# Six row dots moved from the end of the upward phase into the first six items of the downward phase

## The chip, the core and the metric

The kernel runs on one core of a Trainium2 chip. The metric is the time of one execution on the device, in microseconds (us). The engines named below are PE (TensorE: matrix products), DVE (VectorE) and ACT (ScalarE) for elementwise work, POOL (GpSimd), which here issues gathers and stores, and SP (SyncE), which issues the other transfers. Each engine runs its own list of instructions in order; semaphores order work between them. Sixteen DMA engines serve all transfers.

## What is computed

The reference is one step of a decoder layer for 520 tokens (512 of a prompt, 8 samples) of width 1024: modulated norm, a recurrent block and sparse attention, an output projection, then a feed-forward with 16384 experts and a last norm. The change touches the feed-forward alone:

```
s = jnp.einsum('nhpd,hpkd->nhpk', q, subkeys)        # two top-16 lists per head, 8 heads
e = ...                                              # 128 chosen experts for each token
g = jax.nn.softmax(best, axis=-1)
z = jnp.einsum('nd,nhkd->nhk', xc, u_tab[e])         # token times chosen rows of u
act = (jax.nn.gelu(z.astype(jnp.float32)) * g).astype(xc.dtype)
return jnp.einsum('nhk,nhkd->nd', act, v_tab[e])     # weighted sum of chosen rows of v
```

## The kernel before

The feed-forward is done in two ways at once.

**Dense part, 392 tokens.** For all 16384 experts, in 128 blocks of 128, PE computes u times the hidden state (upward phase, `up(b)`, b = 0 to 127), ACT applies GeLU, and the results go to memory. Then, in the downward phase, they are read back, multiplied by a gate that is zero where a token did not choose an expert, and multiplied by v (`down(k)`, k = 0 to 127, accumulated over all k in the eight banks of PE's accumulator memory). One block is called an item. Each 32-bit product is made of three passes of reduced width: high times high, high times low, low times high. So every item needs a high and a low part of its weights, 128x1024 (`raw` -> `uh` by ACT in `high(i)`, then `ul = raw - uh` by DVE in `low(i)`; i = 0 to 127 are blocks of u, 128 to 255 blocks of v) and, downward, of the gated activations (`zin` times the gate `gr` in `gate_item`, `ah` by ACT in `high_a`, `al` by DVE in `low_item`). Rings of four buffers hold `raw`, `uh`/`ul`, `zbuf`, `zin`, `ah`/`al`.

**Sparse part, the other 128 tokens.** One token stands in each partition. For each of its 128 choices, POOL gathers the token's row of u (128 rows of 1024, 512 KB per gather) and DVE multiplies and sums it with the token's hidden state: `dot_rows(n)`, the row dot, which fills column n of `zg`. When all 128 columns are there, ACT applies GeLU (`ag`), DVE multiplies by the softmax weight (`gwt`), POOL gathers rows of v, and DVE adds them up, `add_rows(n)`: vacc += row * ag[n]. The gathers share one ring of four buffers (`xT` in the profile): the gather of u row n waits for dot n-4, the gather of v row n for dot 124+n (n < 4) or for sum n-4.

**What sets the order around the change.** In the last part of the upward phase PE alternates `up` with `quad` products that build the gate; ACT moves them to `stage`, and POOL stores them to `gw` in seven chunks. The last chunk's four stores (3.5 MB) stand in POOL's list behind the gather of u row 121 and ahead of that of row 122. After the last quad PE runs only `up(122)` to `up(127)`, then `down(0)` on. `up(b)` waits for `low(b)`; ACT, after it has taken `up(b)` out, does `high(b + 4)`. DVE's list there is `low(i)` for i = 123 to 127, with two dots (122, 123; 124, 125; 126, 127) behind each of the first three. On SP, the load of raw block i waits for `low(i - 4)`; behind the load of raw block 130 come the wait for all stores of `gw`, the loads of `gr` for items 0 to 3 and of `zin` for item 0, and later those of the next items. At item 8 the saved residual (2 MB, `xspill`) is read in the same list.

Of the kernel before, what the change touches and what calls it, by code (L numbers as in the profile page):

```python
# [16 lines left out]
ACT = mybir.ActivationFunctionType  # L17
AX = mybir.AxisListType
ADD, MUL, SUB, MAX, MIN, EQ = ALU.add, ALU.mult, ALU.subtract, ALU.max, ALU.min, ALU.is_equal

P = 128
# [26 lines left out]
NCH = DN // TC  # L48
# [6 lines left out]
TILE_G = (0, 6, 6, 6, 2)  # L55
PLACED = 8
FIRST_L = (0, 1, 2, 3, PLACED, 4, 5, 6)
CH_U, CH_G = 9, 14
LAST_G = sum(TILE_G) + NCH * CH_G + 4
TAIL_U = 6  # L60
HOT_U = Q_U + sum(TILE_U)
JB = 4
# [29 lines left out]
def build(nc, io):  # L92
    ctx = ExitStack()
    with ctx:
        def sem(name):
            return ctx.enter_context(nc.semaphore(name))

        def sb(name, shape, dt=F32):
            return ctx.enter_context(nc.sbuf_tensor(name, shape, dt))
# [24 lines left out]
        gwt, zg, ag = sb("gwt", [P, P]), sb("zg", [P, P]), sb("ag", [P, P])  # L124
# [141 lines left out]
        S = {n: sem(n) for n in names}  # L266
# [199 lines left out]
        def _(pool):  # L466
# [55 lines left out]
            def gather(n, table, s):  # L522
                pool.indirect_dma_start(  # L523
                    out=gb[:, s, :], out_offset=None, in_=table,
                    in_offset=bass.IndirectOffsetOnAxis(ap=gidx[:, n:n + 1], axis=0)).then_inc(gb_l[s], 16)

            def store_stage(ch, q):

                pool.wait_ge(S["g_moved"], QPC * (ch + 1))
                cols = slice(q * P * TC // PIECES, (q + 1) * P * TC // PIECES)  # L530
                pool.dma_start(io["gw"][ch, :, cols], stage[:, ch % 2, cols]).then_inc(st_l[ch % 2], 16)
# [5 lines left out]
            for n in range(P):  # L537
                if n >= 4:
                    pool.wait_ge(S["ttr_done"], n - 3)
                gather(n, io["u"], n % 4)  # L540
                if n in after_gather:
                    store_stage(*after_gather[n])
                if n == LAST_G - 1:
                    for q in range(PIECES):
                        store_stage(NCH - 1, q)
            v = io["v"].rearrange("a b d -> (a b) d")
# [575 lines left out]
        def _(act):  # L1122
# [8 lines left out]
            def fn(out, in_, f, **kw):  # L1131
                return act.activation(out, in_, f, **kw)  # L1132
# [48 lines left out]
            for n in range(1, ZC):  # L1181
# [12 lines left out]
                b = 2 * (n % 2)  # L1194
# [76 lines left out]
            def high(i):  # L1271

                act.wait_ge(raw_l[i % 4], 16 * (i // 4 + 1))
                if i >= 4:
                    act.wait_ge(S["pe_item"], i - 3)
                fn(uh[:, i % 4, :], raw[:, i % 4, :], ACT.Copy).then_inc(S["hi_done"], 1)

            def gelu(b, bank):
                act.wait_ge(S["pe_item"], b + 1)
                if b >= 4:  # L1280
                    act.wait_ge(zst[b % 4], 16 * (b // 4))
                fn(zbuf[:, b % 4, :], ps[:, bank, 0:DN], ACT.Gelu_apprx_tanh).then_inc(S["gelu_done"], 1)
                high(b + 4)
# [54 lines left out]
            for n in range(QUADS):  # L1338
                move_quad(n)
                for q in after_quad(n % QPC, CH_U):  # L1340
                    b = HOT_U + (n // QPC) * CH_U + q
                    gelu(b, b % 4)
            def high_a(k):
                act.wait_ge(S["mul_done"], k + 1)
                fn(ah[:, k % 4, :], zin[:, k % 4, :], ACT.Copy).then_inc(S["ah_done"], 1)
            for b in range(P - TAIL_U, P):
                if b == P - 1:
                    high_a(0)
                gelu(b, b % 4)
                if b == P - 3:  # L1350
                    act.wait_ge(S["ttr_done"], P)
                    fn(ag[:, :], zg[:, :], ACT.Gelu_apprx_tanh).then_inc(S["zg_gelu"], 1)

            for k in range(P):
                if k >= 4:
                    act.wait_ge(S["pe_item"], P + k - 3)
                if k >= 1:
                    high_a(k)
                if 4 <= k + 1 < P:
                    high(P + k + 1)  # L1360
# [7 lines left out]
        def _(dve):  # L1368
            steps = [0]

            def link(*group):

                for ins in group:
                    steps[0] += 1
                    ins.then_inc(S["dve_step"], 1)
                dve.wait_ge(S["dve_step"], steps[0])

            tt, ts, cp = dve.tensor_tensor, dve.tensor_scalar, dve.tensor_copy
# [138 lines left out]
            for n in range(0, ZC, 2):  # L1517
# [3 lines left out]
                b = 2 * (n % 2)  # L1521
# [201 lines left out]
            for c in range(KD):  # L1723
                dve.wait_ge(S["pe_step"], c + 1)
                b = 2 + 2 * (c % 3)
# [35 lines left out]
            def low(i):  # L1761

                dve.wait_ge(S["hi_done"], i + 1)
                tt(ul[:, i % 4, :], raw[:, i % 4, :], uh[:, i % 4, :].bitcast(F32), SUB).then_inc(S["lo_done"], 1)  # L1764
# [44 lines left out]
            def dot_rows(n):  # L1809

                dve.wait_ge(gb_l[n % 4], 16 * (n // 4 + 1))
                dve.tensor_tensor_reduce(gb[:, n % 4, :], gb[:, n % 4, :], hg[:, :], 1.0, 0.0, MUL, ADD,  # L1812
                                         zg[:, n:n + 1]).then_inc(S["ttr_done"], 1)
# [27 lines left out]
            r, m = slice(0, P), P  # L1841
# [104 lines left out]
            for n in range(QUADS):  # L1946
                ch, i = n // QPC, n % QPC
# [3 lines left out]
                    low(HOT_U + 1 + ch * CH_U + q)  # L1951
                for q in after_quad(i, CH_G):
                    dot_rows(sum(TILE_G) + ch * CH_G + q)
            for n in range(LAST_G - 4, LAST_G):
                dot_rows(n)
            def gate_item(k):
                s, jj = k // JB, k % JB
                if jj == 0:
                    dve.wait_ge(g_l[s % 4], 16 * (s // 4 + 1))
                dve.wait_ge(zl[k % 4], 16 * (k // 4 + 1))  # L1960
                z = zin[:, k % 4, :].rearrange("p (c t) -> p c t", t=TC)
                tt(z, z, gr[:, s % 4, :].rearrange("p (c j t) -> p c j t", j=JB, t=TC)[:, :, jj, :], MUL).then_inc(S["mul_done"], 1)  # L1962

            def low_item(k):
                dve.wait_ge(S["ah_done"], k + 1)
                tt(al[:, k % 4, :], zin[:, k % 4, :], ah[:, k % 4, :].bitcast(F32), SUB).then_inc(S["a_ready"], 1)  # L1966
            for i in range(P - TAIL_U + 1, P):
                low(i)
                for n in range(LAST_G, P)[2 * (i - P + TAIL_U - 1):2 * (i - P + TAIL_U)]:
                    dot_rows(n)  # L1970
            gate_item(0)
            low(P)
            low_item(0)
            dve.wait_ge(S["zg_gelu"], 1)
            link(tt(ag[:, :], ag[:, :], gwt[:, :], MUL))


            def add_rows(n):

                dve.wait_ge(gb_l[n % 4], 16 * (P // 4 + n // 4 + 1))  # L1980
                if n == 0:
                    ts(vacc[:, :], gb[:, 0, :], ag[:, 0:1], None, MUL).then_inc(S["acc_step"], 1)
                else:
                    dve.wait_ge(S["acc_step"], n)
                    stt(vacc[:, :], gb[:, n % 4, :], ag[:, n:n + 1], vacc[:, :], MUL, ADD).then_inc(S["acc_step"], 1)  # L1985
            for k in range(P):
                if k:
                    gate_item(k)
                add_rows(k)
                if k:  # L1990
                    low_item(k)
                if P + k + 1 < 2 * P:
                    low(P + k + 1)
# [137 lines left out]
```

## Time and profile before

| | |
|---|---|
| median of 3 runs | 1822.7 us (1821.66 to 1826.14) |
| profiled execution | 1822.52 us, of which the span of the trace is 1820.0 us |
| PE busy | 1746.2 us, 96% of the span |
| DVE, ACT, POOL busy | 72%, 36%, 19% |
| mean granted clock of PE | 0.974 of full speed |
| DMA | 467.85 MB moved, mean 257 GB/s |

Times in the trace count from the start of the span. The upward phase ends at about 1253 us and the downward phase runs from there to about 1792 us. The chain of work that ended last puts 28% of the span on the downward products (line 1089) and 25% on the upward ones (line 979). Matmul rows overlap in the trace, so what one item costs on PE is read from the distance between the ends of items.

### The profile page before, as it was taken

How to read it: one execution, taken by the hardware profiler on the slowest of the kernel's cores; microseconds unless marked ns; L12 is line 12 of the kernel's file. 1: busy time of each engine (PE TensorE's matmuls, PEld its weight loads, DVE VectorE, ACT ScalarE, POOL GpSimd, SP SyncE). 2: the span in 40 equal slices, each digit the busy share in tenths (PEclk: the TensorE clock that was granted, in tenths of full speed). 3: DMA queues.
4: the chain of work that ended last, by engine and by line, in shares of the span. 5: the costliest groups of instructions: out<-in, count | busy, mean ns of one | idle time of the engine just before them, and what ended most of it. 6: DMA issues, size and time to landing. Idle time of an engine off the chain costs nothing.

```text
span 1820.0 us, 30382 instructions
## 1 busy us (share of the span) xinstructions
PE 1746.2 (96%) x11385; PEld 1626.7 (89%) x11385; DVE 1314.0 (72%) x2978; ACT 647.6 (36%) x1023; POOL 341.5 (19%) x372
## 2 busy tenths in 40 slices
PE   7999998779899999999999999998999999999997
PEld 5688876448799999999999999998999999999997
DVE  0224336662676799998999999956787777777776
ACT  1114422661332234343333333332343333333332
POOL 3101000000000002111333333333222222222220
PEclk9999986899899999999999999998999999999999
DMA  9767654300532147776899999989999999999992
GB/s 345 245 220 278 223 162 161 119 1 1 185 126 85 70 129 270 246 234 205 288 364 365 365 348 339 336 314 371 403 395 330 340 342 335 340 339 330 345 309 78
DMA packets 178952, 467.85 MB, mean 257 GB/s; under 512 B 20515, under 2 KB 92707, under 8 KB 177294
## 3 DMA queue, kind: packets, MB, share of 16 engines
q1 hardware_dynamic: 130974, 290.20, 45.9%
q0 software_dynamic: 45120, 173.61, 26.4%
q10 hardware_dynamic: 2736, 2.49, 0.4%
q8 instruction: 68, 1.11, 0.2%
q14 instruction: 54, 0.44, 0.1%
HBM read 408.86 MB, written 64.17 MB: 260 GB/s over the span
## 4 chain that ended last, share of the span: by engine, by line
PE 85%; DVE 6%; DMA 4%; ACT 2%; issue 1%; ACTq 1%; SPq 0%; POOL 0%; DVEq 0%
PE ps L1089 28%; PE ps L979 25%; PE ps L716 6%; PE ps L966 5%; PE ps L1068 5%; PE ps L919 3%; PE ps L618 2%; ACT arena L1132 1%; PE ps L591 1%; DMA xT<-in_u,gidx 1%; DMA arena<-in_w_in 1%; PE ps L895 1%; PE ps L887 1%; DMA raw<-in_v 1%; DVE arena L1630 1%
## 5 line engine op out<-in xcount | busy, mean ns | idle before, releaser
L1764 DVE TENSOR_TENSOR ul<-raw,uh 128x1024 fp32r<-128x1024 f32 x256 | 311.5, 1222 | 117.8 <-ACT uh L1132 116.3
L979 PE MATMUL ps<-hh,uh 128*128 128x392 f32 x1024 | 358.2, 350 | 8.7 <-DVE ul L1764 8.7
L979 PE MATMUL ps<-hl,uh 128*128 128x392 f32 x1024 | 349.8, 342 | 0.0
L979 PE MATMUL ps<-hh,ul 128*128 128x392 f32 x1024 | 349.0, 341 | 0.0
L1089 PE MATMUL ps<-ah,uh 128*128 128x392 f32 x1000 | 339.6, 340 | 2.5 <-DVE al L1966 2.5
L1089 PE MATMUL ps<-ah,ul 128*128 128x392 f32 x1000 | 341.7, 342 | 0.0
L1089 PE MATMUL ps<-al,uh 128*128 128x392 f32 x1000 | 340.9, 341 | 0.0
L1132 ACT ACTIVATE uh<-raw 128x1024 fp32r<-128x1024 f32 x256 | 269.8, 1055 | 105.6 <-PE ps L1089 91.2
L523 POOL DMA_INDIRECT xT<-in_u,gidx x128 | 148.8, 1163 | 585.6 <-DVE zg L1812 370.1
L523 POOL DMA_INDIRECT xT<-in_v,gidx x128 | 132.4, 1034 | 408.7 <-DVE vacc L1985 388.4
L1132 ACT ACTIVATE zbuf<-ps 128x392 f32<-128x392 f32 x128 | 63.7, 498 | 407.0 <-PE ps L979 407.0
L979 PEld LDWEIGHTS ps<-hh,uh 128*128 128x128 f32 x1024 | 193.3, 189 | 10.9 <-DVE ul L1764 9.3
L979 PEld LDWEIGHTS ps<-hl,uh 128*128 128x128 f32 x1024 | 193.3, 189 | 0.0
L979 PEld LDWEIGHTS ps<-hh,ul 128*128 128x128 f32 x1024 | 193.2, 189 | 0.0
L1089 PEld LDWEIGHTS ps<-ah,uh 128*128 128x128 f32 x1000 | 187.9, 188 | 3.2 <-issue 1.9
L1089 PEld LDWEIGHTS ps<-al,uh 128*128 128x128 f32 x1000 | 187.8, 188 | 0.0
L1089 PEld LDWEIGHTS ps<-ah,ul 128*128 128x128 f32 x1000 | 187.7, 188 | 0.0
L1812 DVE CUSTOM_DVE_ANT_0 xT<-xT,hg 128x1024 f32<-128x1024 f32 x128 | 155.2, 1215 | 22.7 <-DMA xT<-in_u,gidx 22.5
L1985 DVE SCALAR_TENSOR_TENSOR vacc<-xT,ag,vacc 128x1024 f32<-128x1024 f32 x127 | 162.3, 1278 | 0.0
L1132 ACT ACTIVATE ah<-zin 128x392 fp32r<-128x392 f32 x128 | 68.2, 532 | 236.9 <-DVE zin L1962 236.9
L716 PE MATMUL ps<-arena 128*128 128x260 f32 x576 | 132.5, 389 | 2.9 <-DVE arena L1418 2.0
L716 PEld LDWEIGHTS ps<-arena 128*128 128x128 f32 x576 | 109.2, 192 | 20.1 <-DMA arena<-in_w_in 3.1
(355 smaller groups left out, 2221.1 us busy)
## 6 DMA issues: line engine op xcount, KB each, us to landing
raw<-in_uT SPq DMA_DIRECT2D x128, 512.0 KB, 5.1
raw<-in_v SPq DMA_DIRECT2D x128, 512.0 KB, 6.3
zs<-zbuf SPq DMA_DIRECT2D x128, 196.0 KB, 5.3
gw<-stage POOLq DMA_DIRECT2D x28, 896.0 KB, 8.9
gr<-gw SPq DMA_DIRECT2D x32, 784.0 KB, 8.3
zin<-zs SPq DMA_DIRECT2D x128, 196.0 KB, 5.8
arena<-in_ada_w SPq DMA_DIRECT2D x32, 512.0 KB, 4.4
arena<-in_w_in SPq DMA_DIRECT2D x18, 512.0 KB, 6.8
```

The costliest lines, as they stand in the source:

```text
L523: pool.indirect_dma_start(out=gb[:, s, :], out_offset=None, in_=table, in_offset=bass.IndirectOffsetOnAxis(ap=gidx[:, n:n + 1], axis=0)).t ...
L618: last = mm(ps[g * HD:(g + 1) * HD, 2 + 2 * c + h, 1 - m:257 - m], w1p[:, c * 16 + m * 8 + j, :], xv[:, h, :, c, g, j, :], start=(m == 0 a ...
L716: last = mm(ps[:, 2 * (n % 2) + h, 0:HALF], win_w[:, (n % 2) * KD + k, :], hT[:, k, h * HALF:(h + 1) * HALF], start=(k == 0), stop=(k == K ...
L919: last = mm(ps[:, 2 + 2 * (c % 3) + h, 0:HALF], wout[:, k, c * P:(c + 1) * P], zT[:, k, h * HALF:(h + 1) * HALF], start=(k == 0), stop=(k ...
L966: last = mm(ps[:, b + h, 0:HALF], weights[w](k), moving[m](k)[:, h * HALF:(h + 1) * HALF], start=(first and n == 0 and w == 0 and m == 0), ...
L979: last = mm(ps[:, bank, 0:DN], w[x][:, k * P:(k + 1) * P], m[:, k, G0:TOK], start=(k == 0 and x == 0 and m is hh), stop=(k == KD - 1 and x ...
L1068: last = mm(ps[:, 4 + n % 4, t * P:(t + 1) * P], oh[:, n % 6, t * P:(t + 1) * P], oh[:, n % 6, (4 + t) * P:(5 + t) * P], start=True, stop= ...
L1089: last = mm(ps[:, dc, 0:DN], w[:, q, cols], m[:, q, :], start=(first and w is uh and m is ah), stop=False)
L1132: return act.activation(out, in_, f, **kw)
L1764: tt(ul[:, i % 4, :], raw[:, i % 4, :], uh[:, i % 4, :].bitcast(F32), SUB).then_inc(S["lo_done"], 1)
L1812: dve.tensor_tensor_reduce(gb[:, n % 4, :], gb[:, n % 4, :], hg[:, :], 1.0, 0.0, MUL, ADD, zg[:, n:n + 1]).then_inc(S["ttr_done"], 1)
L1985: stt(vacc[:, :], gb[:, n % 4, :], ag[:, n:n + 1], vacc[:, :], MUL, ADD).then_inc(S["acc_step"], 1)
```

## The change

`LATE_G` is 6. The last six dots, 122 to 127, leave the upward phase; one stands in each of the items 0 to 5 of the downward phase, in the place where a row sum stood. ACT's GeLU over `zg` moves from behind `up(125)` to item 6. The row sums begin at item 6; from there each item adds one row, and items 19, 39, 59, 79, 99 and 119 add two, so that 128 are added in all. The code of PE, POOL and SP issues the same instructions in the same order.

```
-LAST_G = sum(TILE_G) + NCH * CH_G + 4
+LATE_G = P - sum(TILE_G) - NCH * CH_G - 4
...
@@ ACT @@
-                if b == P - 3:
-                    act.wait_ge(S["ttr_done"], P)
-                    fn(ag[:, :], zg[:, :], ACT.Gelu_apprx_tanh).then_inc(S["zg_gelu"], 1)
             for k in range(P):
                 if k >= 4:
                     act.wait_ge(S["pe_item"], P + k - 3)
+                if k == LATE_G:
+                    act.wait_ge(S["ttr_done"], P)
+                    fn(ag[:, :], zg[:, :], ACT.Gelu_apprx_tanh).then_inc(S["zg_gelu"], 1)
                 if k >= 1:
                     high_a(k)
...
@@ DVE @@
             for i in range(P - TAIL_U + 1, P):
                 low(i)
-                for n in range(LAST_G, P)[2 * (i - P + TAIL_U - 1):2 * (i - P + TAIL_U)]:
-                    dot_rows(n)
             gate_item(0)
             low(P)
             low_item(0)
-            dve.wait_ge(S["zg_gelu"], 1)
-            link(tt(ag[:, :], ag[:, :], gwt[:, :], MUL))
...
+            def added(k):
+                def rows_until(m):
+                    return max(m - LATE_G, 0) + min(m // 20, LATE_G)
+                return range(rows_until(k), rows_until(k + 1)) if k >= LATE_G else ()
             for k in range(P):
                 if k:
                     gate_item(k)
-                add_rows(k)
+                if k < LATE_G:
+                    dot_rows(P - LATE_G + k)
+                if k == LATE_G:
+                    dve.wait_ge(S["zg_gelu"], 1)
+                    link(tt(ag[:, :], ag[:, :], gwt[:, :], MUL))
+                for n in added(k):
+                    add_rows(n)
                 if k:
                     low_item(k)
                 if P + k + 1 < 2 * P:
                     low(P + k + 1)
```

DVE's list at the end of the upward phase, before, from dot 121 on. L1812 is a dot (the second row reads its sum out), L1764 is `low`:

```order
L1812 ISA xT,zg<-xT,hg 128x1024
L1812 ISA zg 128x1
L1764 TENSOR_TENSOR ul<-raw,uh 128x1024
L1812 ISA xT,zg<-xT,hg 128x1024
L1812 ISA zg 128x1
L1812 ISA xT,zg<-xT,hg 128x1024
L1812 ISA zg 128x1
L1764 TENSOR_TENSOR ul<-raw,uh 128x1024
```

The same place after, up to dot 123. L1962 is `gate_item`, L1966 `low_item`:

```order
L1812 ISA xT,zg<-xT,hg 128x1024
L1812 ISA zg 128x1
L1764 TENSOR_TENSOR ul<-raw,uh 128x1024 x5
L1962 TENSOR_TENSOR zin<-zin,gr 128x392
L1764 TENSOR_TENSOR ul<-raw,uh 128x1024
L1966 TENSOR_TENSOR al<-zin,ah 128x392
L1812 ISA xT,zg<-xT,hg 128x1024
L1812 ISA zg 128x1
L1764 TENSOR_TENSOR ul<-raw,uh 128x1024
L1962 TENSOR_TENSOR zin<-zin,gr 128x392
L1812 ISA xT,zg<-xT,hg 128x1024
L1812 ISA zg 128x1
```

Between dot 121 and the first gated item five `low` now stand with nothing between them, and dot 122 stands behind `low_item(0)`.

DVE's list after at items 18 and 19, where the first doubled sum stands (L1980 is the row sum; before, one stood in each item):

```order
L1980 SCALAR_TENSOR_TENSOR vacc<-xT,ag,vacc 128x1024
L1966 TENSOR_TENSOR al<-zin,ah 128x392
L1764 TENSOR_TENSOR ul<-raw,uh 128x1024
L1962 TENSOR_TENSOR zin<-zin,gr 128x392
L1980 SCALAR_TENSOR_TENSOR vacc<-xT,ag,vacc 128x1024 x2
L1966 TENSOR_TENSOR al<-zin,ah 128x392
```

Of the two sums of item 19 the second stands ahead of that item's `low_item`.

## Rows read from the trace of the kernel before

**Rows 1.** The page's first part: busy time, share and instructions by engine.

```profile
PE 1746.2 (96%) x11385; PEld 1626.7 (89%) x11385; DVE 1314.0 (72%) x2978; ACT 647.6 (36%) x1023; POOL 341.5 (19%) x372
```

**Rows 2.** Stages: length, busy time by engine, granted clock, DMA share, GB/s.

```profile
1216.00:1228.00 12.00, 9.52 (x54) 9.19 (x52) 0.00 (x0) 4.33 (x6) 4.02 (x5) 1.00 0.99 403
1228.00:1240.00 12.00, 7.11 (x25) 7.11 (x26) 8.71 (x13) 0.00 (x0) 7.63 (x5) 0.57 0.85 308
1240.00:1254.00 14.00, 13.02 (x73) 12.69 (x71) 4.65 (x7) 5.54 (x9) 1.68 (x1) 1.00 1.02 387
1254.00:1308.00 54.00, 53.36 (x299) 53.35 (x300) 41.31 (x52) 17.41 (x23) 13.85 (x13) 1.00 1.04 403
1308.00:1312.00 4.00, 3.09 (x18) 2.76 (x17) 3.92 (x5) 1.52 (x3) 0.75 (x1) 1.00 1.04 392
...
1400.00:1700.00 300.00, 300.00 (x1682) 300.00 (x1681) 236.05 (x281) 111.50 (x140) 71.42 (x70) 1.00 0.96 338
```

**Rows 3.** Waits from 1210 to 1260 us: total, times, longest, in us.

```profile
DVE xT L1812 <- DMA xT<-in_u,gidx: 21.1, 3, 15.5
...
PE ps L979 <- DVE ul L1764: 7.4, 1, 7.4
...
PE ps L1089 <- DVE al L1966: 1.6, 1, 1.6
```

**Rows 4.** Timeline of DVE, 1200 to 1320 us: start, length, instruction, [idle before].

```profile
1211.30 1.23 DVE L1812 CUSTOM_DVE_ANT_0 xT<-xT,hg 128x1024 f32<-128x1024 f32 x1 [3.49 <-DMA xT<-in_u,gidx]
...
1212.45 1.22 DVE L1764 TENSOR_TENSOR ul<-raw,uh 128x1024 fp32r<-128x1024 f32 x1
1229.20 1.22 DVE L1812 CUSTOM_DVE_ANT_0 xT<-xT,hg 128x1024 f32<-128x1024 f32 x1 [15.54 <-DMA xT<-in_u,gidx]
...
1231.62 1.22 DVE L1764 TENSOR_TENSOR ul<-raw,uh 128x1024 fp32r<-128x1024 f32 x1
...
1252.31 0.57 DVE L1962 TENSOR_TENSOR zin<-zin,gr 128x392 f32<-128x392 f32 x1 [9.35 <-DMA zin<-zs]
...
1254.41 0.28 DVE L1975 TENSOR_TENSOR ag<-ag,gwt 128x128 f32<-128x128 f32 x1
```

**Rows 5.** Timeline of ACT, the same stretch.

```profile
1212.18 1.05 ACT L1132 ACTIVATE uh<-raw 128x1024 fp32r<-128x1024 f32 x1
...
1225.55 0.50 ACT L1132 ACTIVATE zbuf<-ps 128x392 f32<-128x392 f32 x1 [2.85 <-PE ps L979]
...
1240.18 0.50 ACT L1132 ACTIVATE zbuf<-ps 128x392 f32<-128x392 f32 x1 [13.19 <-PE ps L979]
...
1244.47 0.50 ACT L1132 ACTIVATE zbuf<-ps 128x392 f32<-128x392 f32 x1 [2.84 <-PE ps L979]
...
1245.81 0.30 ACT L1132 ACTIVATE ag<-zg 128x128 f32<-128x128 f32 x1
```

**Rows 6.** The chain that ended last, 1200 to 1320 us: start, length, what.

```profile
1214.01 2.18 POOL gw L531 x4
...
1216.49 12.69 DMA xT<-in_u,gidx
...
1242.28 0.38 SPq L424
...
1242.71 9.50 DMA zin<-zs
...
1254.64 34.56 PE ps L1089 x192
```

**Rows 7.** Issue to landing: the last four stores of gw; then three loads of gr.

```profile
DMA to landing us min/median/max: 7.4/9.9/12.2
...
DMA to landing us min/median/max: 9.0/10.7/13.5
```

**Rows 8.** Timeline of DVE in the settled downward phase.

```profile
1604.46 1.23 DVE L1764 TENSOR_TENSOR ul<-raw,uh 128x1024 fp32r<-128x1024 f32 x1 [0.89 <-ACT uh L1132]
...
1606.08 1.28 DVE L1985 SCALAR_TENSOR_TENSOR vacc<-xT,ag,vacc 128x1024 f32<-128x1024 f32 x1
```

More of the change, by code:

```diff
@@ L542, in _ @@
                     store_stage(*after_gather[n])
-                if n == LAST_G - 1:
+                if n == P - LATE_G - 1:
                     for q in range(PIECES):
@@ L1953, in _ @@
                     dot_rows(sum(TILE_G) + ch * CH_G + q)
-            for n in range(LAST_G - 4, LAST_G):
+            for n in range(P - LATE_G - 4, P - LATE_G):
                 dot_rows(n)
```

## The prediction

> **What bounds the kernel now.** I read the page first, then the table of stages, then the waits, timelines and chain around the border of the two phases. PE is busy for 96% of the span [rows 1], so time can only be won where PE is idle or runs at less than full clock. The stages show where that is. From 1400 to 1700 us PE is never idle at full clock: 1682 products in 300 us are 70.1 items of 24, 4.28 us each [rows 2]. In that stage DMA moves 338 GB/s, and since it reaches 403 from 1254 to 1308 us [rows 2], PE is the bound and the transfers have some 16% to spare. Between 1216 and 1254 us it is otherwise: PE lacks 2.5, 4.9 and 1.0 us in three stages, and the granted clock of the middle one is 0.57 [rows 2].
>
> The waits name the cause: PE waited once, 7.4 us, for `low` of DVE, and once, 1.6 us, for `al`; DVE waited 21.1 us in three pieces for gathered rows of u [rows 3]. In DVE's timeline `low(123)` runs at 1212.45, then dot 122 is idle for 15.54 us and starts at 1229.20, and `low(124)` starts at 1231.62 only [rows 4]. Its input was ready long before: ACT wrote `uh` of block 124 from 1212.18 to 1213.23 [rows 5]. PE had ended `up(123)` at 1225.55, when ACT could take it out [rows 5], and needed `low(124)` from then. So the wait of dot 122 is what PE waits for. The chain says why the row was late: four stores to `gw` at 1214.01 come ahead of the gather of row 122, which is issued at 1216.49 and takes 12.69 us [rows 6].
>
> Two prices follow. The stall itself is 7.4 us. After it the clock is at half (1.2 of 2.4 GHz): `up(124)` runs from about 1232.9 (1225.55 plus 7.4) to 1240.18, 7.3 us, while `up(125)` takes 1244.47 - 1240.18 = 4.29 us [rows 5]. The low clock costs 3.0 us.
>
> At the border the chain has the loads of `gr` and `zin` for item 0, issued at 1242.28 and 1242.71, the second landing 9.50 us later; DVE starts on it at 1252.31 [rows 4, 6], and `down(0)` at 1254.64 [rows 6]: 2.43 us from landed data to PE (from 1252.21). Those loads stood in SP's list behind raw block 130, which waits for `low(126)`, itself delayed by the dots.
>
> **The change part by part.**
>
> *Six dots leave the tail.* DVE then goes from `low(123)` straight to `low(124)`, ready about 1214.9 (1212.45 plus two times 1.22). `low(125)`, `low(126)` and `low(127)` follow ACT's `high`, which follow the ends of PE's items, so each is ready at least one item (4.29 us) ahead of PE. PE does not wait: `up(124)` to `up(127)` run from 1225.5 to 1225.5 + 4 x 4.29 = 1242.7. Before, they ended at 1254.64 - 1.6 = 1253.0. Gain up to here 7.4 + 3.0 = 10.4 us. What hid the dots' own 1.22 us before is no matter; they were no price, their waiting was.
>
> *SP's list moves up.* Raw blocks 128, 129 and 130 are no longer held by late `low`s: they are issued at about 1215, 1220 and 1224; before, the first of them had to wait for `low(124)`, over at 1232.8 [rows 4], and the last stood just ahead of 1242.28 [rows 6]. The next wait in that list, which was over long before, is now the one that ends last: the stores of `gw` must have landed. The row I don't have is how long these stores take with the raw loads beside them. Bounds: alone, the last of four was issued at about 1215.7 (1216.19 less a quarter of 2.18) and took at most 12.2 us, so 1227.9 [rows 6, 7]; at worst every byte of the three raw loads and of two stores of z (2.0 MB, in 4.9 us at 403 GB/s) goes first: 1232.8. I take 1232, close to the late bound, since DMA was full from 1216 to 1228 already (share 0.99) [rows 2] and the raw loads need their 1.6 MB somewhere. The loads of `gr` and `zin` for item 0 then land about 9.9 us after issue, as they did under a full DMA [rows 6]: 1241.9, and `down(0)` could start at 1244.3 by the same 2.43 us. PE is ready at 1242.7. It waits some 1.3 to 1.6 us, as before: the wait keeps its length and moves 10 to 11 us forward. Gain from this term 0.3 us. The early bound (1227.9 and 9.0 us) has no wait at all: gain 1.6. The late bound (1232.8, and 13.5 us, the slowest load of `gr` [rows 7]) gives 1246.3 + 2.4 = 1248.7, a wait of 6.0 us, a loss of 4.4 against the old 1.6, and possibly the low clock again, 3.0 more.
>
> *Dots in items 0 to 5.* A dot of 1.22 us stands where a sum of 1.28 (0.75 in item 0, and 0.28 for `ag` times `gwt`) stood [rows 4, 8]. DVE's item gets no longer. The data: rows 122 to 125 were gathered before item 0; 126 and 127 are gathered after dots 122 and 123, four items ahead of their use, as every v row was. Cost nothing; the cover is the ring of four items, 17 us against a landing of 12.69 at the worst seen [rows 6]. POOL issues two gathers of u and four of v later than before: 3.1 MB leave the crowded stretch before `down(0)`.
>
> *GeLU over zg at item 6.* ACT does it (0.30 us [rows 5]) behind the end of `down(2)`, for which it waits anyway, and DVE's 0.28 follows; PE needs item 6 three items later, 12.8 us. Nothing.
>
> *Six doubled items.* One more sum of 1.28 us in each. In the settled phase DVE is idle 0.89 us per item, waiting for ACT, which waits for `down(k-3)` [rows 8]. So DVE has `al` of item k when PE begins `down(k-2)`, two items or 8.5 us ahead, and the 1.28 us are a delay of 0.4 in the next `low`. The second row was gathered with the ring's usual three to four items of lead. Price 0; if that lead were gone, 1.28 - 0.89 = 0.4 us each, 2.3 in all.
>
> *DMA behind the border.* A gain at the border is only kept if transfers keep up. Before, they were full from 1254 to 1312 us at least, and PE lacked 0.9 us at 1308 to 1312 [rows 2]: the 2 MB residual was ahead of a raw block. Check by bytes: the same work up to `down(0)` without 3.1 MB is 7.9 us less at 390 to 403 GB/s, and the DMA time lost while SP and POOL were held (308 instead of 403 GB/s for 12 us, 387 for 14) is 3.4 us more: 11.3 us. So DMA can be 11.3 us earlier at the border and behind it, against PE's 10.7. They agree to within the guess about the stores; the small stall at item 13 stays as it is.
>
> Here a page of the Trainium skill speaks against the change. "SBUF — State Buffer", in the section on a bandwidth-pool intuition, puts memory to one core at some 358 GB/s and calls it the usual end-to-end bottleneck. Rows of this kernel have 403 over 54 us [rows 2], so the measurement decides here and the sum goes by it. By the page's figure the 55 us from `down(0)` to item 13 would carry 2.5 MB less, an estimate of 6 us of stalls and of 1818 for the time, which would fall into rival D below.
>
> **Sum.** 7.4 (stall) + 3.0 (clock) + 0.3 (border) = 10.7 us. Against the profiled execution, 1822.5 - 10.7 = 1811.8 us; that execution lies 0.2 us under the median of the runs, so the median of the changed kernel is forecast at 1811.9, 0.6% less.
>
> **Rivals.**
>
> *A, the forecast*, border wait between 0.5 and 3 us: 1810.5 to 1813.3. Chance 0.55.
>
> *B, all hidden.* Stores land early, no border wait, and the stall at item 13 goes as well: 1822.7 - 7.4 - 3.0 - 1.6 - 0.9 = 1809.8. For it: 3.1 MB fewer in the queues. Against it: the raw loads beside the stores. 0.18.
>
> *C, the wait moves to the border.* The stores and `gr` come by the late bound: gain 10.4 - 4.4 = 6.0, or 3.0 if the clock falls again: 1816.7 to 1819.7. For it: the three loads of `gr` behind the border took 9.0 us or more each [rows 7]. 0.13.
>
> *D, transfers can't feed the earlier start.* PE begins at 1244, and the raw blocks of items 4 to 14 come late. If no more flowed there than the 338 GB/s of the settled stage, the 55 us up to item 13 would carry 3.6 MB less, 9 us: 1820.8; halfway to 403, 4.5 us: 1816.4. For it: DMA is full in the whole stretch behind the border. Against it: it is full because it runs ahead; need is 338, and 403 flow [rows 2]. 0.07.
>
> *E, slower.* The six doubled items: the second sum waits for its gather, `low_item` stands behind it, and DVE's lead of 8.5 us is spent. It ends on the other side of the old time when each costs PE over 10.7 / 6 = 1.8 us; at 4 us each it would be 24 less 10.7: 1835. Against it: gathers are issued three to four items (12.8 us and more) ahead. 0.04.
>
> *F, the change doesn't do what it says.* PE's wait at 1225 is held by something other than the dots, and is still there: 1822. Against it: `uh` of block 124 was ready 12 us earlier [rows 5]. 0.03.
>
> **How the numbers follow.** Within 0.3% (5.5 us, about what a measurement of this kernel can tell from no change) of 1822.7 means 1817.2 to 1828.2. Below it lie A, B, 0.10 of C and 0.03 of D: faster 0.86. The rest of C (with the low clock) and of D, and F, are the same: 0.10. E is slower: 0.04. The range of 8 in 10 takes in A and B and the first values of C and D: 1808.5 to 1817.5, with 1.3 us under B for its own spread; 0.14 is left above it. The likeliest case's own range is 1810.5 to 1813.3.
>
> **What would show it.** In the changed profile: no wait of DVE for a gather between 1213 and 1243; no wait of PE for `low`; granted clock 1.00 from 1216 to 1244; ends of `up(124)` to `up(127)` 4.29 us apart; `down(0)` at 1244 (1242.7 if B, 1248 if C), held by `al`, behind `zin` of item 0, behind the stores; the raw loads of v from 1215 on; dots of 1.22 us in items 0 to 5 without idle time before them; 4.28 us per item at items 19 to 119. A longer border wait, DVE waiting for `uh` behind raw loads in items 4 to 14, or PE idle at item 19 or 39 would prove me wrong.

## The result and the profile after

The changed kernel takes 1808.59 us (median of 5 runs, 1804.13 to 1810.51), the kernel before 1821.66 us (5 runs, 1814.34 to 1826.14). The difference is 13.1 us; the ratio is 0.9927, 95% interval 0.9904 to 0.9950. Run again on another chip the ratio was 0.9938 (0.9920 to 0.9956), which is 11.3 us less. It is faster.

The stages after, with the columns of [rows 2]:

```profile
1216.00:1228.00 12.00, 12.00 (x69) 12.00 (x68) 3.68 (x3) 4.34 (x6) 4.24 (x4) 1.00 1.03 407
1228.00:1240.00 12.00, 12.00 (x69) 12.00 (x69) 0.00 (x0) 4.34 (x6) 0.00 (x0) 1.00 1.03 403
1240.00:1254.00 14.00, 13.72 (x76) 13.24 (x75) 13.93 (x21) 4.53 (x7) 4.75 (x4) 1.00 1.06 393
1254.00:1308.00 54.00, 54.00 (x302) 53.67 (x302) 41.81 (x55) 19.70 (x27) 12.26 (x12) 1.00 1.04 403
1308.00:1312.00 4.00, 4.00 (x25) 4.00 (x24) 4.00 (x6) 1.69 (x3) 1.60 (x2) 1.00 1.04 406
...
1400.00:1700.00 300.00, 300.00 (x1681) 300.00 (x1681) 241.01 (x285) 111.52 (x140) 80.80 (x74) 1.00 0.96 346
```

The three holes of PE in [rows 2] (2.5, 4.9, 1.0 us) have shrunk to one of 0.3 us, the granted clock is 1.00 throughout, and PE is whole at 1308 us too. The last stage carries one doubled item's gather more per 20 items, 346 GB/s, with PE never idle.

The waits after, 1210 to 1260 us, against [rows 3]: the 15 us wait of a dot and PE's wait for `low` are gone. DVE waits for `zin` of item 0 instead, 12.4 us, and PE for `al` 0.3 us:

```profile
DVE zin L1962 <- DMA zin<-zs: 12.4, 1, 12.4
...
DVE xT L1812 <- DMA xT<-in_u,gidx: 3.4, 1, 3.4
...
PE ps L1089 <- DVE al L1966: 0.3, 1, 0.3
```

DVE's timeline after, against [rows 4]: the `low` of blocks 123 and 124 run one behind the other, those of 125, 126 and 127 wait for ACT alone (125 is shown), then comes the empty stretch, then item 0 with dot 122 behind its `low_item`:

```profile
1211.83 2.36 DVE L1764 TENSOR_TENSOR ul<-raw,uh 128x1024 fp32r<-128x1024 f32 x2
1217.86 1.23 DVE L1764 TENSOR_TENSOR ul<-raw,uh 128x1024 fp32r<-128x1024 f32 x1 [3.68 <-ACT uh L1132]
...
1240.07 0.57 DVE L1962 TENSOR_TENSOR zin<-zin,gr 128x392 f32<-128x392 f32 x1 [12.39 <-DMA zin<-zs]
...
1242.16 1.22 DVE L1812 CUSTOM_DVE_ANT_0 xT<-xT,hg 128x1024 f32<-128x1024 f32 x1
```

The chain that ended last, 1200 to 1320 us, against [rows 6]. It now runs through the landing of the stores of `gw`, 15.61 us, and the load of `zin` for item 0, 8.84 us:

```profile
1206.88 4.30 PE ps L979 x24
...
1213.43 1.65 POOL gw L531 x3
1215.09 15.61 DMA gw<-stage
...
1231.13 8.84 DMA zin<-zs
...
1242.39 77.75 PE ps L1089 x432
```

**Where the time went.** Executions differ ahead of the feed-forward: the first 312 upward products in one piece start at 683.01 us before and at 681.84 after, and in the experiments anywhere from 678.1 to 687.5, though nothing is changed there. I therefore also give the time from that piece to the end of the span, the *feed-forward time*. The rows are in the chain of each kernel, of before

```profile
683.01 56.08 PE ps L979 x312
```

and of after

```profile
681.84 56.07 PE ps L979 x312
```

Before: 1820.0 - 683.01 = 1137.0. After: 1806.9 - 681.84 = 1125.1. The change is worth 11.9 us there. Of the 13.9 us between the two profiled executions, 1.2 lie ahead of it and 0.8 outside the span, where nothing was changed.

### The profile page after: what moved, and what is told of

Same layout as the page of the kernel before. It is cut to its first block, busy times and chain, and to the rows that moved or that the text cites. A ratio compares the mean times of both kernels' runs of the same rounds, so it can differ in the third digit from the quotient of the medians.

```text
span 1806.9 us, 30382 instructions
## 1 busy us (share of the span) xinstructions
PE 1742.5 (96%) x11385; PEld 1623.5 (90%) x11385; DVE 1314.5 (73%) x2978; ACT 647.6 (36%) x1023; POOL 346.7 (19%) x372
## 4 chain that ended last, share of the span: by engine, by line
PE 87%; DVE 6%; DMA 3%; ACT 2%; issue 1%; ACTq 1%; SPq 0%; POOL 0%; DVEq 0%
PE ps L1089 30%; PE ps L979 26%; PE ps L716 6%; PE ps L966 5%; PE ps L1068 5%; PE ps L919 3%; PE ps L618 2%; ACT arena L1132 2%; PE ps L591 1%; PE ps L895 1%; DMA arena<-in_w_in 1%; PE ps L887 1%; DMA gw<-stage 1%; DVE arena L1630 1%; PE ps L988 1%
## 5 line engine op out<-in xcount | busy, mean ns | idle before, releaser
L1764 DVE TENSOR_TENSOR ul<-raw,uh 128x1024 fp32r<-128x1024 f32 x256 | 311.6, 1223 | 119.6 <-ACT uh L1132 108.8
L523 POOL DMA_INDIRECT xT<-in_v,gidx x128 | 138.3, 1081 | 377.0 <-DVE vacc L1980 355.5
L1980 DVE SCALAR_TENSOR_TENSOR vacc<-xT,ag,vacc 128x1024 f32<-128x1024 f32 x127 | 162.5, 1279 | 0.6
L1812 DVE CUSTOM_DVE_ANT_0 xT<-xT,hg 128x1024 f32<-128x1024 f32 x128 | 155.4, 1216 | 5.0 <-DMA xT<-in_u,gidx 4.8
```

What stands on the lines that cost most here:

```text
L523: pool.indirect_dma_start(out=gb[:, s, :], out_offset=None, in_=table, in_offset=bass.IndirectOffsetOnAxis(ap=gidx[:, n:n + 1], axis=0)).t ...
```

## The experiments

Each ratio is to a kernel before that ran on the same chip. "ff" is the feed-forward time, by the same two numbers (span, start of the piece of 312) as above, and "gain kept" is 1137.0 less ff. These two come from one profiled execution of each kernel, not all on one chip, and there is one such trace of the kernel before. The two traces of the changed kernel and those of raw130_later, after_x2_late and doubles_settled lie within 0.3 us of each other (1125.0 to 1125.3); for kernels in which PE stalls nothing shows so narrow a spread.

| kernel | ratio to before, 95% | ff, us | gain kept, us |
|---|---|---|---|
| before | 1 | 1137.0 | 0 |
| changed | 0.9927, 0.9904 to 0.9950 | 1125.1 | 11.9 |
| changed, again | 0.9938, 0.9920 to 0.9956 | 1125.2 | 11.8 |
| two_stay | 0.9989, 0.9975 to 1.0004 | 1134.7 | 2.3 |
| six_in_gap | 0.9963, 0.9947 to 0.9978 | 1132.8 | 4.2 |
| four_in_gap | 0.9949, 0.9931 to 0.9966 | 1130.4 | 6.6 |
| stores_behind | 0.9971, 0.9956 to 0.9986 | 1133.3 | 3.7 |
| raw130_later | 0.9934, 0.9911 to 0.9956 | 1125.2 | 11.8 |
| before_x2_late | 0.9994, 0.9978 to 1.0010 | 1139.0 | -2.0 |
| after_x2_late | 0.9932, 0.9908 to 0.9956 | 1125.3 | 11.7 |
| doubles_together | 0.9975, 0.9961 to 0.9989 | 1133.4 | 3.6 |
| doubles_every_3 | 0.9946, 0.9930 to 0.9961 | 1127.0 | 10.0 |
| doubles_settled | 0.9943, 0.9924 to 0.9961 | 1125.0 | 12.0 |

**The changed kernel again** (label after_again, no edit).

> The changed kernel once more, unedited, as the measure for the three that run with it. If its gain is the stall of PE at the border, the low clock behind it and the small stall at item 13, the ratio to the kernel before lies at 0.9927 again (13 us), within about 0.2%. If half of it was a chance of the runs, it lies at 0.996 or above.

0.9938; the feed-forward time repeats to 0.1 us (1125.1 and 1125.2). PE's small stall at item 13 is there again, at 0.2 us (3.82 of 4 us busy from 1300 to 1304).

**Two dots stay in the tail** (two_stay).

```
             for i in range(P - TAIL_U + 1, P):
                 low(i)
+                if i == P - TAIL_U + 1:
+                    dot_rows(P - 6)
+                    dot_rows(P - 5)
...
-                if k < LATE_G:
-                    dot_rows(P - LATE_G + k)
+                if k < 4:
+                    dot_rows(P - 4 + k)
```

> Dots 122 and 123 stay behind low(123), as before the change; only the last four stand in items 0 to 3, and the sums begin at item 4. Theory 1 (what counts is that no low stands behind a dot that waits for a late gather): dot 122 still waits some 15 us, PE waits 7 us for low(124) at half clock afterwards, and at most 2 us of the gain are left: ratio 0.998 to 1.0. Rival (what counts is the 3.1 MB of gathers that leave the stretch before the downward phase): four of six dots moved, four gathers of v left the stretch, so half or more of the gain stays: ratio 0.996 or less.

Theory 1 holds. Two of six dots bring back nearly the whole stall; PE's timeline has

```profile
1236.97 0.69 PE L979 MATMUL ps<-hh,uh 128*128 128x392 f32 x1 [7.33 <-DVE ul L1764]
```

and 2.3 of 11.9 us are left, though four dots were moved and four gathers of v left the stretch. By number of dots or by bytes alone it would have kept two thirds. Besides the lines shown, the edit lets the sums begin at item 4 and doubles four items.

**All six behind the last `low`** (six_in_gap) **and four of them there** (four_in_gap).

```
             for i in range(P - TAIL_U + 1, P):
                 low(i)
+            for n in range(P - LATE_G, P):
+                dot_rows(n)
             gate_item(0)
```

In four_in_gap the range ends at P - 2, and dots 126 and 127 stand in items 0 and 1. The sums begin at item 1 and item 2; one and two items are doubled.

> All six dots stand behind low(127) and ahead of the first gated item, where DVE is idle for 12.4 us in the changed kernel; sums begin at item 1. No low stands behind a dot any more, but two gathers of u and up to four of v (3.1 MB) are back in the stretch before the downward phase. Theory 1: no stall of PE in up(124) to up(127), full clock; the first downward product is held by the last dots and by later zin: 2 to 5 us later than in the changed kernel, so 8 to 11 us of the 13 are kept: ratio 0.994 to 0.9955. Rival (bytes): the gain goes but for the order: ratio 0.997 or more.

> Dots 122 to 125 stand behind low(127), in DVE's idle stretch; 126 and 127 in items 0 and 1; sums begin at item 2. Four gathers (2.1 MB) are back ahead of the downward phase, but none of the dots there has to wait for a gather that was issued late. Theory 1: as the changed kernel to within 2 us, and if anything slower by the bytes (zin of item 0 lands 1 to 3 us later, and a small stall at item 13 comes back): ratio 0.9925 to 0.994. Rival (bytes): half of the gain is gone: ratio 0.996.

In their traces both missed what I expected on the slow side: 4.2 and 6.6 us kept, where 8 to 11 and about 11 were expected. The ratios are kinder and don't settle it: 0.9963 (6.7 us) and 0.9949 (9.3 us), with intervals that reach into the ranges expected. `up(124)` to `up(127)` have no stall in either, so the order did its work, but something else costs time. In six_in_gap the dots themselves wait for their gathers, the first 4.64 us and the last 2.78 us; the last gather is issued at 1232.67 only and takes 8.21 us. Counted from the piece of 312, the first downward product starts at 566.2 us, against 560.5 in the changed kernel; PE waits 6.0 us there and then runs at half clock:

```profile
1232.67 8.21 DMA xT<-in_u,gidx
...
1244.37 85.71 PE ps L1089 x465
```

with these stages of 4 us (columns as in [rows 2]):

```profile
1240.00:1244.00 4.00, 0.00 (x0) 0.00 (x0) 3.10 (x5) 1.36 (x3) 1.02 (x1) 0.85 1.03 403
1244.00:1248.00 4.00, 3.63 (x11) 3.66 (x12) 3.96 (x7) 1.24 (x3) 0.90 (x1) 0.50 1.06 396
```

In four_in_gap no stall is long, but there are five for `al`, 4.5 us in all:

```profile
PE ps L1089 <- DVE al L1966: 4.5, 5, 1.5
```

at full clock, at 1244 to 1252, 1268 to 1276 and 1304 to 1308 us, while DMA carries 388 to 401 GB/s. Dot 122 waits 5.06 us there for its gather, though that was not issued late. The kernel has four gathers (2.1 MB) more ahead of the border than the changed kernel; at 400 GB/s these are 5.2 us. Its trace lost 5.3 us: 0.7 up to the first downward product, 4.2 in the downward products and 0.5 in the work behind them, which the edit doesn't touch. So its loss is about the time of these bytes. That the bytes made it is argued, not shown, since no run moved bytes alone: in six_in_gap the sum fits as well (3.1 MB are 7.9 us, 7.7 were lost), though there 5.7 us were lost before the first downward product, and the clock fell. What the two runs do show is that the order takes the stall of 7.4 us away by itself, and that their traces keep less of the gain than the changed kernel's.

**The stores behind the gathers, dots where they were** (stores_behind, from the kernel before).

```
-                if n == LAST_G - 1:
+                if n == LAST_G + 3:
                     for q in range(PIECES):
                         store_stage(NCH - 1, q)
```

> The kernel before, with one edit: the last four stores of gw stand behind the gather of row 125 and no longer ahead of that of row 122. All dots stay where they were. If it is the stores that made row 122 late, dot 122 no longer waits 15 us, low(124) and low(125) are in time and the stall of 7.4 us with its low clock is gone or down to 2 us; gathers 126 and 127 now stand behind the stores, so low(126) can come some us late, and the stores land 5 us later, which holds gr and zin: first downward product 3 to 8 us earlier than in the kernel before, ratio 0.996 to 0.999. If the gather is late for another reason (its own issue, the bytes in flight), dot 122 waits on and the ratio is 1.0.

It was the stores that made row 122 late: dots 122, 123 and 124 run without a wait, dot 125 waits 3.28 us, and the long wait has moved to dot 126, whose gather now stands behind the stores. PE's stall is 4.8 us, for `low(126)`, with a clock of 0.50 behind it. DVE's timeline:

```profile
1218.80 1.22 DVE L1812 CUSTOM_DVE_ANT_0 xT<-xT,hg 128x1024 f32<-128x1024 f32 x1
...
1226.73 1.23 DVE L1812 CUSTOM_DVE_ANT_0 xT<-xT,hg 128x1024 f32<-128x1024 f32 x1 [3.28 <-DMA xT<-in_u,gidx]
...
1240.22 1.23 DVE L1812 CUSTOM_DVE_ANT_0 xT<-xT,hg 128x1024 f32<-128x1024 f32 x1 [11.12 <-DMA xT<-in_u,gidx]
```

The first downward product starts 4.1 us earlier than in the kernel before (567.5 against 571.6, counted from the piece of 312), within the 3 to 8 us expected. By the trace 3.7 us are won, a third of the change; by the ratio 0.9971, 5.3 us (2.6 to 8.0).

**A raw block held back** (raw130_later).

```
                 store_z(b)
-                load_raw(b + 8)
+                if b < P - 6:
+                    load_raw(b + 8)
...
             load_z(0)
+            load_raw(P + 2)
             store_z(P - 5)
```

> The changed kernel with the load of raw block 130 (0.5 MB) moved behind the wait for the stores of gw and the loads of gr and zin for item 0. It measures how much the raw loads hold up the stores. If the stores share the DMA engines with what SP issues, they land 1.3 us earlier (512 KB at 403 GB/s) than 1230.7, and zin of item 0 with them, some 1 to 2 us earlier. If the two queues don't hold each other up, nothing moves. PE is ready at 1242.1 and waits 0.3 us in the changed kernel, so the time gains 0.3 us at most, if block 130 itself is in time for high(130) at 1238: ratio 0.9925 to 0.994.

The stores did not land earlier: from POOL's first store (1216.04) to SP's load of `gr` (1232.86) are 16.8 us; in the changed kernel 17.3 (1213.43 to 1230.71), again 16.7 (1215.62 to 1232.32). The 1.3 us that the block's bytes would take do not show against a spread of 0.6 us between two traces of the changed kernel: a block issued 10 us after the stores didn't hold them up by its bytes. PE's wait of 0.3 us at the border was gone, but one of 0.7 us at item 13 was there instead, and nothing was won.

**The residual at item 60** (before_x2_late, after_x2_late).

```
-                if k == 8:
+                if k == 60:
                     sp.wait_ge(S["pe_item"], P)
```

> The kernel before, with the load of the saved residual (2 MB) moved from item 8 to item 60 of the downward phase; nothing else. If that load is what makes raw block 141 late, PE's idle 0.9 us at the start of item 13 is gone and the time is 0.9 us less: ratio 0.9995, too little for the runs, to be read in the trace. If the stretch behind the border is short of bytes anyway, the stall stays at an item nearby.

> The changed kernel with the load of the saved residual moved from item 8 to item 60. There PE had no stall at item 13, so nothing is to be won: ratio to the kernel before as the changed kernel's, 0.9927, within 0.1%. DVE's wait of 8 us for uh around 1287 to 1295 us is gone, which shows how near the stall was.

In the kernel before, PE now waits for `al` once in the whole downward phase, at the border, and no more at item 13. That load made the raw block late: with it at item 8, ACT waits 7.19 us for a raw block just ahead of item 13 (8.00 us in the changed kernel), and with it at item 60 no wait of ACT for raw data there is over 1.81 us, in either kernel. PE's waits in before_x2_late:

```profile
PE ps L979 <- DVE ul L1764: 8.5, 2, 7.2
PE ps L1089 <- DVE al L1966: 2.9, 1, 2.9
```

The trace's time was not less: the load of `zin` for item 0 took 11.09 us instead of 9.50, PE waited 2.9 us at the border, and the granted clock fell to 0.75 there. The edit changes nothing that is issued before the border, so this is a difference between two executions. Of the 2.0 us lost, 1.2 lie ahead of the first downward product, 0.4 in the downward products (the low clock, less the stall at item 13 that is gone) and 0.4 behind them. With the change, moving the load is worth nothing (0.9932), and DVE's long wait for `uh` is gone, both as expected.

**The doubled items** (doubles_together: items 7 to 12; doubles_every_3: 7, 10, 13, 16, 19, 22; doubles_settled: 60 to 65). The first of them, in the function `rows_until`; in the others the last term is `max(m - 5, 0) // 3` and `max(m - 60, 0)`:

```
-                    return max(m - LATE_G, 0) + min(m // 20, LATE_G)
+                    return max(m - LATE_G, 0) + min(max(m - 7, 0), LATE_G)
```

> The changed kernel with its six doubled items next to each other, items 7 to 12, where the transfers are full and the residual is loaded, instead of 20 apart. My theory: a second sum costs DVE 1.28 us; six in a row are 7.7 us on an engine that in that stretch idles some 15 us and has a lead of 8.5 us over PE, so PE loses 0 to 2 us: ratio 0.9925 to 0.994. Rival (the lead is smaller than it looks, and a second sum waits for its gather): each costs PE 1.3 us or more, 8 us in all: ratio 0.997 or more.

> The changed kernel with its six doubled items next to each other at items 60 to 65, in the settled stage, where the transfers have some 16% to spare and nothing else is loaded. At items 7 to 12 the same six cost 8 us in the trace. If the crowd (full transfers, residual) made that price, here it is 0 to 1 us. If the ring of four gather buffers makes it (two rows per item leave a gather two items, 8.6 us, from issue to use), DVE waits for gathers of v here too, though they land in some 7 us; the price is 1 to 4 us, since six doubled items ask for 460 GB/s against 403.

> The changed kernel with its doubled items at 7, 10, 13, 16, 19 and 22: in the crowded stretch, but never two in a row. If the crowd makes the price of a doubled item, much of the 8 us stays (bytes: 3.1 MB more before item 22, 7.9 us at 400 GB/s, less the lead that is there, so 3 to 7 us). If it is the ring of gather buffers under two rows per item, the price is under 1 us, since DVE needs five rows in three items.

Next to each other in the crowded stretch they cost 8.3 us of feed-forward time (1133.4 - 1125.1): the price that I had given to none. DVE waits for gathers of v, 4.8 us in three waits, PE 5.3 us for `al` in three, and the clock falls to 0.58 behind the longest (4.0 us). The two sums of item 11 in DVE's timeline, each behind a wait, and the gather of the second in the chain:

```profile
1294.04 1.28 DVE L1980 SCALAR_TENSOR_TENSOR vacc<-xT,ag,vacc 128x1024 f32<-128x1024 f32 x1 [2.61 <-DMA xT<-in_v,gidx]
1296.60 1.28 DVE L1980 SCALAR_TENSOR_TENSOR vacc<-xT,ag,vacc 128x1024 f32<-128x1024 f32 x1 [1.27 <-DMA xT<-in_v,gidx]
```

```profile
1284.93 11.64 DMA xT<-in_v,gidx
```

The same six in the settled stage cost nothing, although DVE waits for gathers there too, 2.2 us in two waits: the lead covers it. Every third item in the crowd, they cost 1.9 us, one wait of PE of 2.8 us behind the residual, at item 13, which is doubled there, and no wait for a gather. So the ring alone makes no price, and the crowd alone a small one (less than the 3 to 7 us expected). Together they do: two rows in each item leave a gather half the time, two items or 8.6 us, and the one above took 11.64 us to land. How much of this crowd is the residual was not tried.

## Why the prediction came out as it did

The forecast was 1811.9 us; the measured median is 3.3 us less. At 1808.59 it stands at the lower end of the range, 1808.5, and by the ratio to its own before (0.9927 x 1821.66 = 1808.4) just under it. The direction and the main mechanism held; two terms of the sum were too small, the border (0.3 us, measured 1.3) and item 13 (nothing, measured 0.7 to 0.9). What happened is close to case B of the rivals, "all hidden", which had a chance of 0.18: of the border wait 0.3 us are left.

*The stall and the clock, 7.4 + 3.0 us.* Right, and shown three ways: both are gone in the changed kernel, the stall comes back with two dots (two_stay, 7.3 us), and the wait of dot 122 goes when the stores stand elsewhere, leaving a stall of 4.8 us for a later `low` (stores_behind).

*The border.* "It waits some 1.3 to 1.6 us, as before" was the step that failed. PE waited 0.3 us, so the term was 1.3 us and not 0.3; in six more traces with all six dots in items 0 to 5 that wait is between 0 and 0.7 us. I had the stores land at 1232 and `zin` 9.9 us after; they landed at 1230.7 and it took 8.84 us, 9.3 when run again. My way to the 1232 let the bytes of three raw blocks delay the stores nearly in full; by raw130_later the third, issued 10 us behind them, did not delay them measurably. Why the loads of `gr` and `zin` came a microsecond faster stays open.

*The stall at item 13* "stays as it is": wrong by 0.7 to 0.9 us. It was 0 in the profile and 0.2 when run again; in raw130_later it was 0.7. One of my signs of being wrong did appear, DVE waiting for `uh` behind a raw load in items 4 to 14:

```profile
1295.01 1.23 DVE L1764 TENSOR_TENSOR ul<-raw,uh 128x1024 fp32r<-128x1024 f32 x1 [8.05 <-ACT uh L1132]
```

The kernel before has the same wait (7.24 us, with PE's 0.9 us behind it). In the changed kernel PE lost nothing by it, so the sign was badly chosen: it tells how near a stall is, not that there is one.

*The bytes.* I checked that the transfers could be 11.3 us earlier against PE's 10.7, and took that as agreement. four_in_gap, with four gathers ahead of the border again, lost time in small stalls under a full DMA, so the margin behind the border is thin. Rival D did not come true, but what it fears is near.

The page of the Trainium skill that spoke against the change ("SBUF — State Buffer", in the section on a bandwidth-pool intuition, 358 GB/s from memory to a core) is not borne out by these traces: 403 GB/s over the 54 us behind the border, before and after. That page of the Trainium skill gives the figure as a memory stack's 716 GB/s divided by two cores; this program runs on one, and no run here has a second core busy.

*The doubled items.* Nothing at 20 apart, as forecast: the stage from 1400 to 1700 us has PE at 300.00 us of 300. Rival E needed late gathers in the doubled items; doubles_together is the case in which that happens. (E's own sum is off by one: 24 less 10.7 is 13.3, so 1836 and not 1835.)

*The sum.* 7.4 + 3.0 + 1.3 + 0.9 = 12.6 us by PE's own rows, against 11.9 of feed-forward time; 0.6 of the difference lies in the upward phase ahead of the border (from the piece of 312 products to the end of `up(120)` are 528.8 us before, 1211.78 - 683.01, and 529.4 after, 1211.21 - 681.84), and I can't attribute it. That leaves 12.0. Of the 3.3 us by which the median undercuts the forecast, 1.2 are these terms (11.9 against 10.7); the other 2.1 lie outside the feed-forward time, where nothing was changed, and with five executions or fewer on each side they are chance. On the other chip the ratio of 0.9938 gives 11.3 us, and 1811.4 against the 1822.7 of the forecast, inside the likeliest range.

*The range.* It kept 1.3 us under case B for spread. Single executions of one kernel spread over 6 us (changed, 5 runs) to 12 us (before, 5 runs); in the profiled ones the feed-forward starts anywhere within 9 us. The forecast rested on three runs of before, from 1821.66 to 1826.14, which did not show that.

No version here beats the changed kernel: at the border 0.3 us are left, and doubles_settled and after_x2_late are the same within their intervals.

## What to carry to other kernels

A wait for a slow transfer costs what stands behind it in its engine's list, not what it does itself: ask of each such wait which neighbour the critical engine needs next, and let that go first. Where PE is then freed, count bytes up to the point where it needs them: in a stretch where the DMA was full, gathers put off past the border were worth about their transfer time here. When put-off work is caught up later, spread it: one extra row per 20 items is free, six in a row in a crowded stretch gave back two thirds of the gain.

## What the runs showed of the hardware

The granted clock after a wait of PE: in the 13 traces, from 1205 us to the end of the downward products, it fell to the lower of its two levels (0.50 in stages of 2 to 4 us) after every wait of 4.0, 4.8, 6.0 and 7.2 to 7.4 us, and stayed at 1.00 after all waits up to 1.6 us. Of two waits of nearly the same length, 2.9 us (before_x2_late) was followed by a stage at 0.75 and 2.8 us (doubles_every_3) by none. PE had stalled 7.2 us some 20 us before the first and not at all since 1205 us before the second; whether that matters is not shown. The two stages:

```profile
1256.00:1260.00 4.00, 2.12 (x7) 2.15 (x8) 3.96 (x7) 1.89 (x3) 1.01 (x1) 0.75 1.11 375
```

```profile
1304.00:1308.00 4.00, 2.94 (x16) 2.94 (x17) 4.00 (x6) 1.83 (x3) 2.65 (x2) 1.00 1.05 389
```

So a stall of some 3 us has a price of either size, which a forecast should carry as two cases.

The last stores of `gw` took 12.2 us at most to land before [rows 7]. In the changed kernel, where SP issued two more raw blocks (1 MB) and two stores of z in the first 8 us beside them, the last of them was waited for until 15.61 us after POOL had issued it (15.04 when run again).
